# A decoder step on one core: expert weights loaded in longer rows, and some down blocks multiplied in fp32 as they landed

## The reference, cut

```python
def swiglu(x, w_gate, w_up, w_down):
    return (jax.nn.silu(x @ w_gate) * (x @ w_up)) @ w_down

def moe_swiglu(x, router, w_gate, w_up, w_down):
    logits = (xt @ router).astype(jnp.float32)
    top_vals, top_idx = lax.top_k(logits, TOP_K)
    gates = jax.nn.softmax(top_vals, axis=-1)
    combine = jnp.sum(jax.nn.one_hot(top_idx, N_EXPERTS, dtype=jnp.float32) * gates[..., None], axis=1)
    for e in range(N_EXPERTS):
        y_e = swiglu(xt, w_gate[e], w_up[e], w_down[e])
        y = y + combine[:, e:e + 1] * y_e.astype(jnp.float32)
```

## Time and profile before

| What | us |
|---|---|
| Median of 3 runs | 1490.39 |
| Lowest, highest run | 1489.25, 1491.16 |
| Span of the profiled execution | 1489.3 |
| PE busy in the span | 1403.9 (94%) |
| DVE busy | 1323.4 (89%) |
| ACT busy | 1104.7 (74%) |
| Mean rate of the DMA | 312 GB/s |

### The profile page before, as it was taken

How to read it: one execution, slowest core, us unless ns; L and a number is a source line. 1 busy time by engine, 2 the same in 40 slices (tenths; PEclk the granted TensorE clock), 3 DMA queues, 4 the chain that set the end, 5 groups by cost and what they waited for, 6 DMA issues and landing times.

```text
span 1489.3 us, 39853 instructions
## 1 busy us (share of the span) xinstructions
PE 1403.9 (94%) x17570; PEld 1151.0 (77%) x17570; DVE 1323.4 (89%) x1315; ACT 1104.7 (74%) x1032; POOL 123.7 (8%) x162
## 2 busy tenths in 40 slices
PE   9999999999999999899999999999999898798786
PEld 7788878888788888697777788788877776766563
DVE  3999997555669999899999999999999999999997
ACT  4797755544458766688888878888878988978884
POOL 2411025000143001100000000000000000000001
PEclk9999999999999999999999999999999999999898
DMA  9654558456554637899999999999999999999993
GB/s 315 243 170 157 180 193 269 139 170 239 171 183 141 196 127 266 325 352 386 412 409 395 411 407 395 411 406 402 410 405 412 411 407 411 410 403 410 411 393 133
DMA packets 141347, 464.85 MB, mean 312 GB/s; under 512 B 8234, under 2 KB 10410, under 8 KB 126800
## 3 DMA queue, kind: packets, MB, share of 16 engines
q1 hardware_dynamic: 138960, 457.21, 80.4%
q0 software_dynamic: 1920, 4.55, 1.0%
q10 hardware_dynamic: 288, 0.48, 0.1%
HBM read 460.79 MB, written 2.89 MB: 311 GB/s over the span
## 4 chain that ended last, share of the span: by engine, by line
PE 52%; DVE 34%; DMA 5%; issue 5%; ACT 3%; POOL 1%; DVEq 0%; ACTq 0%
PE ps L869 16%; PE ps L870 16%; PE ps L871 16%; DVE w_lo L2284 14%; DVE w_lo L2287 7%; DMA stage<-in_moe_w_up 2%; PE ps L975 2%; DVE w_lo L1754 2%; ACT w_hi L1663 2%; DMA stage<-in_w_in 1%; DVE arena L1871 1%; DVE arena L1882 1%; POOL x L796 1%; DVE arena L2302 1%; DVE arena L2322 1%
## 5 line engine op out<-in xcount | busy, mean ns | idle before, releaser
L869 PE MATMUL ps<-arena,w_hi 128*128 128x128 f16 (+7 forms) x3952 | 564.5, 214 | 15.0 <-issue 10.1
L870 PE MATMUL ps<-arena,w_hi 128*128 128x128 f16 (+7 forms) x3952 | 564.3, 214 | 7.7 <-issue 7.7
L871 PE MATMUL ps<-arena,w_lo 128*128 128x128 f16 (+7 forms) x3952 | 564.3, 214 | 5.1 <-issue 5.1
L869 PEld LDWEIGHTS ps<-arena,w_hi 128*128 128x128 f16 x3952 | 386.1, 99 | 27.7 <-issue 15.8
L871 PEld LDWEIGHTS ps<-arena,w_lo 128*128 128x128 f16 x3952 | 386.2, 99 | 13.7 <-issue 8.3
L870 PEld LDWEIGHTS ps<-arena,w_hi 128*128 128x128 f16 x3952 | 386.2, 99 | 12.8 <-issue 4.8
L869 PE MATMUL ps<-xhl,w_hi 128*128 128x264 f16 x1088 | 300.4, 276 | 8.9 <-DVE xhl L1812 3.6
L871 PE MATMUL ps<-xhl,w_lo 128*128 128x264 f16 x1088 | 300.3, 276 | 0.0
L870 PE MATMUL ps<-xhl,w_hi 128*128 128x264 f16 x1088 | 300.3, 276 | 0.0
L1754 DVE SCALAR_TENSOR_TENSOR w_lo<-stage,w_hi 128x2048 f16<-128x2048 f32 (+1 forms) x94 | 209.1, 2246 | 80.9 <-ACT w_hi L1359 80.8
L1359 ACT ACTIVATE w_hi<-stage 128x2048 f16<-128x2048 f32 (+1 forms) x94 | 172.2, 1853 | 75.2 <-PE ps L871 62.0
(11 more groups left out here) (339 smaller groups left out, 1973.7 us busy)
## 6 DMA issues: line engine op xcount, KB each, us to landing
stage<-in_moe_w_up SPq DMA_DIRECT2D x64, 1024.0 KB, 14.0
stage<-in_moe_w_down SPq DMA_DIRECT2D x48, 1024.0 KB, 14.4
stage<-in_w_in SPq DMA_DIRECT2D x43, 1024.0 KB, 5.3
stage<-in_moe_w_gate SPq DMA_DIRECT2D x34, 1024.0 KB, 10.0
mixer_only<-in_moe_w_up SPq DMA_DIRECT2D x32, 1024.0 KB, 13.6
arena<-in_moe_w_gate SPq DMA_DIRECT2D x32, 1024.0 KB, 13.5
mixer_only<-in_moe_w_gate SPq DMA_DIRECT2D x23, 1024.0 KB, 13.5
mixer_only<-in_moe_w_down SPq DMA_DIRECT2D x16, 1024.0 KB, 14.3
```

The lines of the kernel that those rows point to most:

```text
L869: mm(out, ah, bh, start=start, stop=False, skip_group_check=True)
L870: mm(out, ah, bl, start=False, stop=False, skip_group_check=True)
L871: return mm(out, al, bh, start=False, stop=stop, skip_group_check=True)
```

## The change

Three things change in the expert part; the mixer and the dense layer stay.

- **Pieces.** Hidden columns are in two groups, of four and of three columns of 512. A gate or up piece is one row tile of 2048 columns (8 KB rows, 1 MB) in group 0 and of 1536 columns (6 KB rows, 768 KB, in a home of 1 MB) in group 1. A visit has 46 pieces: gate 0 and up 0 (8 each), gate 1 (8), six down pieces of group 0, up 1 (8), two down pieces of group 0, six of group 1.
- **Down blocks in fp32.** `STRAIGHT` names, for visits 4 to 7, one, two, three and two of the seven columns whose two down pieces aren't split at all: PE multiplies the fp32 product by the fp32 weights straight from their home. These pieces take no slot; their home is given back when PE has multiplied them, not when they are split. "Six ahead" now counts split pieces alone (`ahead`).
- **Order and banks.** Gate 0 and up 0 both use banks 0 to 3, up after Silu has read them; gate 1 uses 0 to 2 and up 1 banks 3, 6 and 7. ACT and DVE do the Silu, the products and the splits of values at places written out (`SILU_AT`, `UP_AT`, `HI_AT`, `LO_AT`, `ADD_AT`). The y halves lie in the tiles of the hidden values' halves. The gather of the next visit's tokens uses banks 0 to 3. In the last visit the residual rows are all made before the down pieces of group 1.

```diff
-BLOCKS = [[c for c in (b, b + 1) if c < NC] for b in range(0, NC, 2)]
+GROUPS = [[0, 1, 2, 3], [4, 5, 6]]
+COLUMN_BANK = {("g", 0): [0, 1, 2, 3], ("u", 0): [0, 1, 2, 3], ("g", 1): [0, 1, 2], ("u", 1): [3, 6, 7]}
+STRAIGHT = {**{v: () for v in range(NE)}, 4: (6,), 5: (5, 6), 6: (4, 5, 6), 7: (3, 6)}
...
+    return (run("g", 0, 0, KT) + run("u", 0, 0, KT) + run("g", 1, 0, KT) + run("d", 0, 0, 6) + run("u", 1, 0, KT) +
+            run("d", 0, 6, 8) + run("d", 1, 0, 6))
...
+def is_straight(i):
+
+    kind, g, q = visit_order()[i % VISIT]
+    return kind == "d" and GROUPS[g][q // 2] in STRAIGHT[i // VISIT]
...
+SILU_AT, UP_AT, HI_AT, LO_AT = (7, 24), (14, 36), (16, 38), (16, 38)
+ADD_AT, TURNED_AT, SELECT_AT, GATHER_AT = (8, 11), 17, 19, 38
...
+        def ahead(v, q):
+
+            i = v * VISIT + q
+            s = SPLIT_BEFORE[i] + SLOTS
+            return SPLIT_LIST[s] - v * VISIT if not is_straight(i) and s < SPLIT_ROUND else None
...
         def visit_piece(e, m):
-            width = 512 * len(BLOCKS[b])
-            k = KT // n_pieces(b)
-            return (w[0, e, q * k * P:(q + 1) * k * P, f:f + width]
-                    .rearrange("a (k p) n -> (a p) k n", p=P)), k, width
+            return (w[0, e, q * P:(q + 1) * P, f:f + width_of(m)]
+                    .rearrange("a (k p) n -> (a p) k n", p=P)), 1, width_of(m)
...
+        def home_left(at, m):
+
+            if is_straight(at[1] * VISIT + m):
+                return multiplied(at, m)
+            return S["lo_done"], split_done(at, m)
...
             def down(at, g, q0, q1):
+                    if is_straight(i):
+                        pe.wait_ge(*up_taken(at, g, c))
+                        pe.wait_ge(*landed_in(r, i))
+                    else:
+                        pe.wait_ge(*values_split(at, g))
+                        pe.wait_ge(S["lo_done"], split_done(at, m))
...
+                            if is_straight(i):
+                                w = HOMES[home_of(r, i)][:, k * D + half * 512:k * D + half * 512 + 512]
+                                t = mm(ps[0:cap, b, :], h_e[:, c, cols], w, start=start, stop=stop, skip_group_check=True)
...
             def last_visit(at):
 
                 up_to_gather(at)
-                down(at, NB - 1)
-                residual_rows(2, [columns_read(b, at, 3) for b in (0, 2)])
+                down(at, 0, 6, 8)
+                residual_rows(1, [up_taken(at, 1, 0)])
+                residual_rows(2, [up_taken(at, 1, 1)])
+                down(at, 1, 0, 6)
...
             def visit(at):
                 for q in range(VISIT):
                     if q == 0 and not first_visit(at):
                         y_lo(at)
+                    if q in ADD_AT and not first_visit(at):
+                        scatter_add(at, ADD_AT.index(q))
+                    for g in range(NG):
+                        if q == UP_AT[g]:
+                            up(at, g)
+                        if q == LO_AT[g]:
+                            values_lo(at, g)
...
+                    m = ahead(at[1], q)
+                    if m is not None:
+                        lo_v(at, m)
```

More of the change, by code:

```diff
@@ L223 @@
 PER_VISIT = [4, 4, 4, 4, 3, 3, 3, 4]
[L226 removed]
+FREED = [4, 0, 3, 1, 3, 1, 1, 1]
 FIRST_FILLS = [0, 0, 0, 0, 2, 2, 2, 2]
@@ L464, in so_far, with split_done, in_groups, hi_of @@
             return r * (NE * each) + (v * each + n)
+        def split_done(at, m):
+            r, v = at
+            return r * SPLIT_ROUND + (split(PRE) + SPLIT_BEFORE[v * VISIT + m + 1])
+        def in_groups(at, g, each, more):
+            r, v = at
+            counts = [(u, h, each(u, h)) for u in range(NE) for h in range(NG)]
+            return r * sum(n for _, _, n in counts) + (more + sum(n for u, h, n in counts if (u, h) < (v, g)))
+        def hi_of(v, g):
+            return min(1, len(by_split(v, g)))
+        def lo_of(v, g):
+            return len(by_split(v, g))
+        def values_split(at, g):
+            return S["e_split"], in_groups(at, g, lo_of, 1 + lo_of(at[1], g))
+        def values_free(at, g):
+            return S["e_split"], in_groups(at, g, lo_of, 1)
         def free_of(name):
@@ new lines, in as_loaded, with gate_up_tile, width_of @@
+        def as_loaded(where, width):
+            return where[:, 0:width].rearrange("p (c two) -> p two c", two=2)
+        def gate_up_tile(t, slot, i, j, width):
+            o = (j % 2) * (width // 2) + P * (2 * i + j // 2)
+            return t[:, slot, o:o + P]
+        def width_of(m):
+            kind, g, q = order[m]
+            return PIECE if kind == "d" else 512 * len(GROUPS[g])
+        def ahead(v, q):
+            i = v * VISIT + q
+            s = SPLIT_BEFORE[i] + SLOTS
+            return SPLIT_LIST[s] - v * VISIT if not is_straight(i) and s < SPLIT_ROUND else None
@@ L667, in _, with visits @@
                 load(*pre_piece(n), n)
-            def visits(r, first=False):
+            def visits(r):
                 for v in range(NE):
@@ new lines, in gate_up, with down @@
+            def gate_up(at, kind, g):
+                for q in range(KT):
+                    if first_visit(at) and (kind, g) == ("g", 0) and q in (0, 4):
+                        for b in ((6, 1), (7, 3))[q // 4]:
+                            pe.wait_ge(*in_visit(bank_free, b, at, -1))
+                    piece(at, kind, g, q)
+                    if (kind, g, q) == ("u", 0, 2) and not first_visit(at):
+                        scatter(at, 1)
+            def down(at, g, q0, q1):
+                r, v = at
+                cap = CAPS[v % NE]
+                for q in range(q0, q1):
+                    m = order.index(("d", g, q))
+                    i = v * VISIT + m
+                    slot = slot_in(i)
+                    c = q // 2
+                    if is_straight(i):
[3 more added lines that the diff above has]
+                        pe.wait_ge(*values_split(at, g))
+                        pe.wait_ge(S["lo_done"], split_done(at, m))
```

427 lines of the change are left out of this document (207 added, 220 removed).

## The result

| | before | after |
|---|---|---|
| median of 4 runs, us | 1490.78 | 1540.72 |
| lowest, highest | 1489.25, 1493.85 | 1539.06, 1542.78 |
| span of the profiled execution | 1489.3 | 1537.0 |

The ratio is 1.0332, 95% interval 1.0317 to 1.0346: the change makes the kernel 50 us slower. The forecast was 1498 us with a range from 1480 to 1508. The sign was right and the size wrong by a factor of six.

A forecast was written before the change was run, and what follows sets the result against it. DVE was taken to pace visits 4 to 6, PE visit 3, loads visit 7. From 1489.3: +3 banks, +0.9, +2.1, +3.9, −4.2 for visits 4 to 7, −1.4 tail, +3.4 clock = 1497.0; plus 1.1, 1498.1 us; range 1480 to 1508.

The forecast's parts named there:

- shared banks: Gate and up sharing banks makes PE wait for Silu and product: 1 us each in visits 0, 2, 3; bounds 0 and 8.
- visit 4: Expert visit with 96 tokens: forecast 104.9 us against 104.0 before, paced by PE's down run after the late low halves.
- visit 5: Expert visit with 80 tokens: forecast 105.2 us against 103.1, with six down pieces of 19.0 us after M + 86.2.
- visit 6: Expert visit with 72 tokens: product behind four more splits, then six fp32 pieces of 3.45 us; 106.7 against 102.8 us.
- visit 7: Last expert visit, 64 tokens: forecast 101.3 us against 105.5, since nothing waits for loads there.
- tail: After PE's end: moved residual rows let the first output matmul start sooner, 17.2 us becoming 15.8.
- clock, on top: After PE idles in visits 5 and 6 the granted clock drops, costing 1.7 us twice, 3.4 us; bounds 0 and 7.
- The new order: Visits 4 to 7: six down pieces need the last values, formed at place 36; low halves at 38; expected price of change.
- M: The moment PE ends a visit's last down piece; the forecast times the next visit's steps from it.
- Homes: Late return of fp32 blocks' homes: the load waiting for visit 6's last one is covered; 1:1 cost beyond 14 us.
- An fp32 piece: Unsplit down piece on PE: four 512-column matmuls, 3.45 us, 0.86 more than f16's 2.59; bounds 2.59 and 3.5.
- loads with the longer rows: Gate and up loads with 8 and 6 KB rows: about 0.1 us saved per megabyte, some 3 us of 108 a visit.

The follow-up runs named there:

- e6: Changed kernel with the first visit's operation that reads the ranks' bank moved ahead of two low halves: 1531.57 us, against 1540.7 for the changed kernel.
- e3: Changed kernel with no fp32 block, group-1 product at step 34 and its fp16 and low halves at 36: 1503.99 us (1.0086 to before).
- e1: Changed kernel with no down block in fp32; rows, shared banks and order kept: 1524.18 us (1.0215 to before).
- e2: Changed kernel, fp32 blocks included, with group-1 product moved from step 36 to 34 and its halves from 38 to 36: 1510.53 us (1.0125 to before).
- e5: Changed kernel with no fp32, but the homes of the same 16 pieces held until TensorE has multiplied them: 1523.60 us.
- e11: Changed kernel with no fp32 block, product and halves early, and homes of the sixteen pieces held until TensorE has multiplied them: 1504.43 us.
- e10: Changed kernel, fp32 blocks included, with the group-1 product alone at step 34, its halves staying at 38: 1545.71 us (1.0352 to before).
- e16: Changed kernel with product and halves early and fp32 blocks in visits 4 to 6 only, none in visit 7: 1506.82 us.
- e13: Changed kernel without fp32, product and halves early, ranks' bank read early, DVE's additions and group-0 product one place forward: 1496.62 us (1.0032 to before).
- e12: Changed kernel with no fp32 block, product and halves early, and ranks' bank read early: 1497.84 us.
- e17: Changed kernel, fp32 blocks included, product left at step 36, its fp16 and low halves moved from 38 to 36: 1538.89 us.

## Why the prediction was right in sign and wrong in size

The steps of the forecast, with what the profiled spans measured (1537.0 − 1489.3 = 47.7 us):

| step | forecast | measured |
|---|---|---|
| visits 0 to 3, "shared banks" | +3 (0 to 8) | +21.9 (10.6, 6.0, 1.5, 3.8) |
| visit 4 | +0.9 | +4.5 |
| visit 5 | +2.1 | +7.6 |
| visit 6 | +3.9 | +12.9 |
| visit 7 | −4.2 | +1.3 |
| tail | −1.4 | −0.5 |
| clock, on top | +3.4 | inside the visits |

**The step that failed first is "Shared banks: in PE's visits (0, 2, 3) I take 1 us each".** It priced the direct hand-overs (Silu, then up; product, then the next gate) and left out two others. The direct ones came out near the price: PE's waits for ACT's Silu and for the group-0 product at gate and up pieces are 2.6 and 3.8 us over visits 1 to 6, and 2.0 us in visit 0. One that was left out is the ranks' bank in visit 0, 4.0 us of waiting and, with the clock, 7.4 us (e6). I hadn't listed who holds banks 2 and 3 when the first visit starts. The other is the group-1 product for the gather's last quarter. I had this chain in the text ("The first product frees bank 3, the last quarter of the gather runs"), but used it only for visits 4 to 6, which I held to be DVE's, and not for visits 1 to 3. e3 against e1, both without fp32, shows it there: 107.7 to 103.1, 117.2 to 116.0 and 106.7 to 104.5 us.

**"The new order. This is where I expect the price" was the right place.** The mechanism is shown: product and values' halves stand too late in DVE's list, PE waits for the one or the other, and both early give 30.2 us back (e2). The term was too small because I summed the time that DVE is busy up to the product, as if it never waited on the way, and did so for visits 4 to 7 alone. In visit 5 the product came at M + 82.5 (1269.86 after 1187.4), where I had M + 80.2, and the four f16 down pieces behind it (48 matmuls, from 1271.12 to the next start at 1284.12) took 13.0 us where I had counted 10.4. These 2.3 and 2.6 us are nearly all of the 5.4 by which visit 5 exceeded its forecast of 105.2. The 2.6 are the lower clock, which the forecast had as a term of its own, at 1.7 us a visit: right in kind and somewhat small.

**Visit 6.** I wrote "place 36 comes behind 38, 39 and the next visit's 0 and 1; M + 71.2 + 8.8": the order was right, the two pieces were assumed to be there. ACT gets them at 1378.45 and 1380.94, as they land, DVE waits 4.3 us for the first, and the product starts at M + 87.2 instead of M + 80.0. That is 7.2 of the 9.0 us over the forecast of 106.7; the lower clock after the idle 7.84 us is most of the rest. The premise "*Homes* of fp32 blocks are given back after the multiplication ... covered" was half right. Without fp32 pieces in them, held homes cost nothing in either order (e5, e11). With them loading does stop: the page's holes of 370, 368 and 313 GB/s lie there. The load that I had checked, the one that waits for the last of the six homes, came as forecast: it landed at 1419.86, 6.2 us after M, and was covered. What I hadn't checked were the pieces behind the held ones. The stop at visit 5's four homes took 4.6 us from the stream, and six fp32 pieces that aren't split brought the turn of the next visit's pieces 0 and 1 forward to a place ahead of the product; there the stock was used up. With the product early the late landing costs little: e10's visit 6 is 106.0 us and e2's 104.0, with all six fp32 pieces.

**Visit 7** was forecast at 101.3, with the product at M + 79.6. It came at M + 84.1 (1497.72), since DVE waited 4.4 us in all for ACT's high halves on the way, and ACT for PE; without fp32 and with the late order (e1) the visit takes 106.6 us as well. The two fp32 pieces of column 3 (38 and 39) don't wait for the product, and I let them run beside the splits. PE came to them only at M + 78.5 (1492.13), so their 7.0 us, two sets of residual rows (3.9) and 17.3 us of down pieces stand one after another: 106.7, as measured. With the early order and f16 pieces there the visit takes 105 us (e3, e16), with fp32 111 (e2). Loads did no harm in this visit, as forecast: nothing waits for a load at its end.

**What held.** An fp32 piece costs 3.43 us against 2.59; a 1536-column half 1.75; loads with the longer rows run faster: 418 GB/s in e13's visits 4 to 6 where the earlier trace rows have 408 to 410. The Trainium skill (DMA: Bandwidth & Descriptors, "Measured") asks for at least 1 MiB a DMA. The 768 KB loads, several queued, land 1.88 us apart, which is the same 418 GB/s, so this trace doesn't bear the rule out. The faster loads' gain is visible in e13: visit 0's loads end 10 us later than before (705.9 against 696.2 us), and by the last landing (1462.1 against 1462.3) the faster stream has made that up. That visit 0's loads end later because 14 homes of smaller pieces hold less of a visit's weights is my reading, which no run shows. The gain then is worth nothing, because eight down pieces and the residual rows lie behind the last up piece at the end.

**How the 50 us divide,** from the medians one edit after another: 30.2 the late product and halves (10.0 of it only together with fp32), 6.5 the fp32 blocks by themselves, 6.2 the ranks' bank, 1.2 the additions (within the spread), and 5 left over. Taken in another order the shares change: fp32 first is 16.5, the ranks' bank alone 9.2. The left-over lies behind the last landing in visit 7, where PE has 24.8 us of work behind the last up piece and had 17.0 before. That the grouping of four and three columns makes it is argued from the rows and not shown by a run, since I made no kernel with another grouping. Nor does a run take the longer rows or the smaller pieces by themselves.

What stays open: why e12's visit 0 ended at 742.4 and e13's at 738.0. Their gate-0 windows had a granted clock of 0.91 and 1.00, and the gather's 48 matmuls ahead of them took 310 and 219 ns already; I found no wait of PE that explains it.

## What to carry to other kernels

Where an order is written by hand, ask of every small operation that others wait for: what stands ahead of it in its engine's list, and what does that wait for? A product of 1 us stood for 10 us behind two splits of weights for later work, and counting only what the list's busy time adds up to hid it. When a wait is removed, look for the next one on the same engine before the gain is booked: product alone and halves alone gave nothing (5 us worse, and no change beyond the spread), both together 30 us. And when an engine other than the bottleneck is relieved by lengthening the bottleneck's turn, price the piece at the end of the program, where nothing runs beside it.

## What the runs showed of the hardware

A wait of PE can cost more than its length: 4.0 us of waiting in visit 0 came with a granted clock of 0.92 over the following 22 us and 0.93 over the next 23, so 7.4 us in all. It is not the same each time. In e17, with the same two waits, the second of these windows was at 1.00, and in e6 the wait of 2.0 us from 642.7 left the clock at 1.00. An fp32 matmul of 512 columns shows as two records of 592 ns and takes 0.86 us of PE (3.43 us for the four of a piece), against 0.65 us for the three f16 matmuls that do the same product in halves (2.59 us for 12). It is a third dearer, and equally so for 64, 72, 80 and 96 tokens.
